# Two transformer blocks on one core: value projection from the raw input, router logits from the raw residual, and the affine part moved behind the gather

## The chip, the cores and the metric

The kernel runs on one core of a Trainium2 chip. The metric is the time on the device, in microseconds, of one execution. PE is the matrix engine, DVE the vector engine, ACT the scalar engine, POOL the general-purpose engine, and SP the engine whose queue issues the transfers.

## The reference

Input x is 1024 tokens of width D = 1024, in fp32. Two blocks run one after the other.

```python
def rmsnorm(x, g): return x * rsqrt(mean(x*x, -1) + EPS) * g
# block 1
h = rmsnorm(x, attn_pre_norm)
proj = h @ w_in                       # window attention, forget attention, latent attention
qm = rmsnorm(c_q, q_latent_norm) @ w_uq       # c_q: 256 columns of proj
kv = rmsnorm(c_kv, kv_latent_norm) @ w_ukv    # c_kv: 128 columns
x = x + rmsnorm(mixed @ w_out, attn_post_norm)
x = x + rmsnorm((gelu(gate) * up) @ w_down, ffn_post_norm)
# block 2: c is one vector
sh1, sc1, gt1, sh2, sc2, gt2 = split(silu(c) @ w_ada + b_ada)
h = rmsnorm(x, g_mix) * (1 + sc1) + sh1       # windowed attention and a short convolution
x = x + gt1 * (concat(att, conv) @ w_out)
h2 = rmsnorm(x, g_ffn) * (1 + sc2) + sh2
aff = softmax(h2 @ w_router)                  # 16 experts
g, idx = top_k(aff.T, 128)                    # each expert picks its 128 tokens
y = (silu(h2[idx] @ w_gate[e]) * (h2[idx] @ w_up[e])) @ w_down[e] * g
x = x + gt2 * scatter_add(y, idx)
out = rmsnorm(x, g_final)
```

## The kernel before

The activations lie in SBUF as 8 tiles (k) of 128 features by 1024 tokens, tokens along the free axis. Every large product is made in three passes, high x high, low x high and high x low, where a "high" is a copy rounded to fp32r (made on ACT) and a "low" is the rest (a subtraction on DVE or POOL). Each engine has its own program, written out by hand; semaphores alone join them. All transfers but the gathers and scatters are issued by SP, in order.

**Start.** SP loads x in four pairs of tiles (L507), then the value weights (L509), then the modulation weights in 8 tiles (`adaA`). ACT squares x, DVE sums the squares (`squares`, `sums`, L1950), PE makes the mean with a matrix of ones (`mean(0)`, L682), ACT the root, DVE the inverse on the diagonal of a matrix (L1963), PE spreads that over all partitions (`spread(0)`, L689), and only then DVE scales x (L2006), ACT rounds it (L1430) and DVE takes the rest (L2011). PE's order is: `keep_clock(10)`, 20 products whose result is not used (L675); mean; bias flips (L788); spread; the modulations of tiles 0 to 3 (L770, 32 rows); the value products (L812 to L814, 8 units of token block by half, 24 products each); the modulations of tiles 4 to 7; then the 13 tiles of the input projection (L826 to L828). DVE and ACT each empty one half of a projection tile. POOL makes the low part of the value weights in one piece (L2611).

**Latent norms.** The sums of squares of the latent columns are averaged at projection tiles 3 and 5 and spread at 4 and 6.

**Output projection and router.** The second output projection has 16 parts of 24 products (`output_part2`, L947 to L949); parts 0 to 7 are the first half of the tokens, 8 to 15 the second. DVE adds each to the residual (`gated`, L2437). The normed, scaled and shifted input hT is made on DVE and ACT (L2444, L1694). From it PE makes the logits (L1210), and for each of the 8 token blocks two transposes, one of the residual and one of hT (`row_turn`, L1201). ACT empties those (L1835) and SP stores them to DRAM as rows (L609), to which the routed row's affinities are added. After the softmax DVE ranks them in 16 rounds of 8 (L2487), finds each token's position and writes the indices; POOL gathers each expert's 128 rows (L2758).

**Experts.** An expert is 24 items: 8 k-tiles of gate, of up and of down. An item is 6 products of 128x512 (L1299 to L1301). ACT rounds its weight tile into one of RING = 4 buffers (`part_high`, L1875), DVE takes the rest (`part_low`, L2543); PE's item waits for that, and ACT's next write into the buffer waits for PE's item four before. Within an expert, PE turns the next expert's gathered rows ahead of its first up item (`turn_rows`, L1308), and ACT and DVE turn them into operands ahead of their own item 4:

```python
def columns(e, b):                      # ACT, at i == 4
    act_e.wait_ge(s_xt, e + 1)
    act_e.activation(x_hi[:, b]..., banks(4, D), ACT.Copy).then_inc(s_xhi, 1)
...
if not last and i == 4:                 # DVE
    columns_low(e + 1, 1 - b)
```

## Time and profile before

| what | value |
| --- | --- |
| median of 3 runs | 2589.3 us (2589.24 to 2589.64) |
| profiled execution, its own time | 2590.66 us |
| its span, first to last instruction | 2588.8 us |
| mean granted clock of PE | 0.975 |
| busy share: PE, DVE, ACT, POOL | 95%, 62%, 48%, 27% |
| chain that ended last | PE 72%, issue 11%, DVE 8%, POOL 4%, ACT 4% |

A share of busy time is a mean over the whole program. The stage from about 2000 us on, the experts, is 23% of the span and has other limits than the projections before it, so each stage is read by itself. In the rows further down, times count from the start of the span; a row of the timeline has start, duration, engine, line, operation, output and inputs, shapes, the number of instructions it groups, and in brackets how long the engine was idle before, and what ended that.

### The profile page before, as it was taken

How to read it: one execution, taken by the hardware profiler on the slowest of the kernel's cores; microseconds unless marked ns; L12 is line 12 of the kernel's file. 1: busy time of each engine (PE TensorE's matmuls, PEld its weight loads, DVE VectorE, ACT ScalarE, POOL GpSimd, SP SyncE). 2: the span in 40 equal slices, each digit the busy share in tenths (PEclk: the TensorE clock that was granted, in tenths of full speed). 3: DMA queues.
4: the chain of work that ended last, by engine and by line, in shares of the span. 5: the costliest groups of instructions: out<-in, count | busy, mean ns of one | idle time of the engine just before them, and what ended most of it. 6: DMA issues, size and time to landing. Idle time of an engine off the chain costs nothing.

```text
span 2588.8 us, 32543 instructions
## 1 busy us (share of the span) xinstructions
PE 2452.7 (95%) x11378; PEld 1918.5 (74%) x11378; DVE 1610.7 (62%) x2439; ACT 1254.0 (48%) x1852; POOL 689.7 (27%) x396
## 2 busy tenths in 40 slices
PE   8999899999999999999999999999997999999996
PEld 5787567777778788777778777765764888888884
DVE  5032887756643367665432635588247999999997
ACT  4121554434543323343433421376344888888886
POOL 1222100113434477334456222121220110111100
PEclk9999999999999999999999999999998999999997
DMA  7100000022222264222223111000138999999996
GB/s 279 49 33 17 34 1 1 1 114 82 82 82 97 97 230 146 80 82 84 95 98 114 66 65 49 33 1 1 67 117 316 402 387 386 397 386 390 396 361 219
DMA packets 86601, 384.06 MB, mean 148 GB/s; under 512 B 7980, under 2 KB 9180, under 8 KB 71520
## 3 DMA queue, kind: packets, MB, share of 16 engines
q1 hardware_dynamic: 81744, 365.25, 37.5%
q0 software_dynamic: 4752, 17.43, 2.5%
q8 instruction: 63, 1.03, 0.2%
q14 instruction: 42, 0.34, 0.0%
HBM read 361.60 MB, written 21.05 MB: 148 GB/s over the span
## 4 chain that ended last, share of the span: by engine, by line
PE 72%; issue 11%; DVE 8%; POOL 4%; ACT 4%; DMA 1%; POOLq 0%; SPq 0%; DVEq 0%; ACTq 0%
PE ps L947 10%; PE ps L949 10%; PE ps L948 10%; PE ps L1299 7%; PE ps L1301 7%; PE ps L1300 7%; POOL w_lo L2667 4%; PE ps L756 3%; PE ps L902 2%; PE ps L826 2%; PE ps L828 2%; PE ps L827 2%; PE ps L748 2%; PE ps L1149 1%; PE ps L770 1%
## 5 line engine op out<-in xcount | busy, mean ns | idle before, releaser
L2667 POOL TENSOR_TENSOR w_lo<-arena,w_hi 128x1024 fp32r<-128x1024 f32 x188 | 462.7, 2462 | 746.4 <-ACT w_hi L1544 742.2
L2543 DVE TENSOR_TENSOR e_lo<-arena,e_hi 128x1024 fp32r<-128x1024 f32 x384 | 454.2, 1221 | 45.4 <-ACT e_hi L1875 34.1
L1875 ACT ACTIVATE e_hi<-arena 128x1024 fp32r<-128x1024 f32 x384 | 404.1, 1062 | 103.1 <-PE ps L1301 103.1
L1544 ACT ACTIVATE w_hi<-arena 128x1024 fp32r<-128x1024 f32 x188 | 198.4, 1055 | 362.9 <-PE ps L949 362.9
L947 PE MATMUL ps<-h_hi,w_hi 128*128 128x512 f32 x848 | 342.6, 404 | 21.4 <-POOL w_lo L2667 11.7
L948 PE MATMUL ps<-h_lo,w_hi 128*128 128x512 f32 x848 | 335.9, 396 | 0.0
L949 PE MATMUL ps<-h_hi,w_lo 128*128 128x512 f32 x848 | 335.9, 396 | 0.0
L947 PEld LDWEIGHTS ps<-h_hi,w_hi 128*128 128x128 f32 x848 | 162.9, 192 | 66.1 <-issue 28.1
L1299 PE MATMUL ps<-e_hi,x_hi 128*128 128x512 f32 x512 | 202.2, 395 | 3.0 <-DVE x_lo L2538 2.6
L1301 PE MATMUL ps<-e_lo,x_hi 128*128 128x512 f32 x512 | 199.5, 390 | 0.0
L1300 PE MATMUL ps<-e_hi,x_lo 128*128 128x512 f32 x512 | 199.3, 389 | 0.0
L949 PEld LDWEIGHTS ps<-h_hi,w_lo 128*128 128x128 f32 x848 | 162.6, 192 | 35.3
L948 PEld LDWEIGHTS ps<-h_lo,w_hi 128*128 128x128 f32 x848 | 163.3, 193 | 33.6 <-issue 1.2
L2234 DVE SCALAR_TENSOR_TENSOR arena<-ps,cols,arena 128x511 f32<-128x511 f32 x88 | 63.8, 746 | 198.0 <-ACT arena L1631 198.0
L947 PE MATMUL ps<-a_hi,w_hi 128*128 128x512 f32 x352 | 138.0, 392 | 3.5 <-DVE arena L2248 3.5
L948 PE MATMUL ps<-act_lo,w_hi 128*128 (+1 forms) x352 | 137.6, 391 | 0.0
L949 PE MATMUL ps<-a_hi,w_lo 128*128 128x512 f32 x352 | 137.6, 391 | 0.0
L1950 DVE TENSOR_TENSOR arena<-arena 128x512 f32<-128x512 f32 (+2 forms) x85 | 85.7, 1008 | 72.7 <-ACT arena L1371 68.6
L1631 ACT ACTIVATE arena<-ps,cols 128x512 f32<-128x512 f32 x88 | 63.6, 773 | 136.5 <-PE ps L949 135.7
L2781 POOL DMA_INDIRECT residual_rows<-arena,tiny x15 | 27.3, 1821 | 356.7 <-DVE arena L2550 356.7
L1299 PEld LDWEIGHTS ps<-e_hi,x_hi 128*128 128x128 f32 x512 | 96.2, 188 | 22.4 <-DVE x_lo L2538 2.9
L1301 PEld LDWEIGHTS ps<-e_lo,x_hi 128*128 128x128 f32 x512 | 96.1, 188 | 20.3
(372 smaller groups left out, 5094.4 us busy)
## 6 DMA issues: line engine op xcount, KB each, us to landing
arena<-in_w_up SPq DMA_DIRECT2D x108, 1024.0 KB, 7.0
arena<-in_w_down SPq DMA_DIRECT2D x86, 1024.0 KB, 7.2
arena<-in_w_gate SPq DMA_DIRECT2D x64, 1024.0 KB, 9.4
arena<-in_w_in SPq DMA_DIRECT2D x18, 1024.0 KB, 4.8
arena<-in_w_out SPq DMA_DIRECT2D x16, 1024.0 KB, 4.7
arena<-in_w_ada SPq DMA_DIRECT2D x12, 1024.0 KB, 12.1
arena<-in_w_ada SPq DMA_DIRECT2D x24, 512.0 KB, 6.8
routed_rows<-arena SPq DMA_DIRECT2D x8, 520.0 KB, 2.6
```

The costliest lines, as they stand in the source:

```text
L756: i = pe.matmul(ps[:, value_bank(w, isdense(w)), 0:HD], probsT[w % 2][:, j * P:(j + 1) * P], group(w)[2](w % 8, j), start=(j == 0), stop=( ...
L947: pe.matmul(out, w_hi[:, q, w], hi, start=start, stop=False)
L948: pe.matmul(out, w_hi[:, q, w], lo, start=False, stop=False)
L949: return pe.matmul(out, w_lo[:, q, w], hi, start=False, stop=stop)
L1299: pe.matmul(out, hi[:, k, :], e_hi[:, r, w], start=(k == 0), stop=False)
L1300: pe.matmul(out, lo[:, k, :], e_hi[:, r, w], start=False, stop=False)
L1301: m = pe.matmul(out, hi[:, k, :], e_lo[:, r, w], start=False, stop=(k == KT - 1))
L1544: act_e.activation(w_hi[:, q, :], slot[c][:, q * D:(q + 1) * D], ACT.Copy).then_inc(s_whi, 1)
L1875: act_e.activation(e_hi[:, (2 * sl + a) % RING, :], slot[sl][:, a * D:(a + 1) * D], ACT.Copy).then_inc(s_ehi, 1)
L1950: v.tensor_tensor(sm[:, 0:n], sm[:, 0:n], sqs[k % 2][:, 0:n], ALU.add).then_inc(s_add, 1)
L2543: v.tensor_tensor(e_lo[:, r, :], slot[sl][:, a * D:(a + 1) * D], e_hi[:, r, :].bitcast(F32), ALU.subtract).then_inc(s_elo, 1)
L2667: gp.tensor_tensor(w_lo[:, q, :], slot[c][:, q * D:(q + 1) * D], w_hi[:, q, :].bitcast(F32), ALU.subtract).then_inc(s_wlo, 1)
```

## The change

It has three parts.

**First input projection from the raw input.** SP loads the value weights first, then x. ACT rounds x times the norm's gain, without the inverse root, and DVE takes the rest in one operation. PE runs 6 times 2 unused products in place of 10 times 2, then the value products, k outermost over four units, then the other four; mean and spread stand among these. The inverse root is applied where results are emptied: as a scale of one number a row for the values (`v_tile`), and as a product with a row for the 13 tiles (`first_tile`), whose both halves DVE now empties. The low part of the value weights is made in two halves, on DVE and POOL. All modulations and flips come behind the values.

**Latent norms** are averaged and spread one tile later.

**Router.** The logits come from the raw residual, with router weights scaled by the gain; the inverse root and the shift of the logits are applied on 128x64 values (`affinity_shifted`). hT is gone, and so are `spread` and the 16 scaling and 16 shifting operations. A token block needs one transpose (`row_turn`), emptied twice on ACT, raw and times the inverse root (`rows_out`). The rows gathered are normed but lack gain and shift: `columns` on ACT applies those in 8 operations before the rounding, for each expert. The unused products ahead of the first expert are gone; parts of `second_gate` stand there. Some weights load earlier.

```diff
+            sp.dma_start(wv, T["w_in_v"]).then_inc(extra, 16)
             for i in range(4):
...
+                sp.dma_start(x0_pairs[i], T["xT"][:, 2 * i:2 * i + 2, :]).then_inc(xl[i], 16)
...
-            keep_clock(10)
-            mean(0)
-            pe.wait_ge(s_bias, 16)
-            bias_turned(range(2))
-            spread(0)
-            bias_turned(range(2, 4)).then_inc(s_flip, 1)
+            keep_clock(6)
...
+            pe.wait_ge(s_n1, 2)
+            for k in range(KT):
+                if k == KT // 2:
+                    pe.wait_ge(s_ilo, 1)
+                pe.wait_ge(s_nhi, k + 1)
+                for u in range(4):
+                    value_product(u // 2, u % 2, k, False)
+                pe.wait_ge(s_h, k + 1)
+                for u in range(4):
+                    m = value_product(u // 2, u % 2, k, True)
...
-                if t in (3, 5):
-                    mean(1 if t == 3 else 2)
                 if t in (4, 6):
-                    spread(1 if t == 4 else 2)
+                    mean(1 if t == 4 else 2)
+                if t in (5, 7):
+                    spread(1 if t == 5 else 2)
...
+            def logits(half, k):
+
+                pe.wait_ge(eva if k % 2 else evv, T_OUT2 + 4 * half + k // 2 + 1)
...
+                m = pe.matmul(ps[0:NE, 7, :], wr_scaled[:, k, :], xT[:, k, half * HALF:(half + 1) * HALF], start=(k == 0), stop=(k == KT - 1))
...
-            output_part2(KT, {4: lambda: mean(12)})
-            output_part2(KT + 1, {2: lambda: spread(12)})
-            for i in range(2):
-                output_part2(KT + 2 + i, {1: lambda: row_turn(2 * i), 5: lambda: row_turn(2 * i + 1)})
-            output_part2(KT + 4, {0: lambda: logits(0), 6: lambda: logit_rows(0)})
-            output_part2(KT + 5, {5: lambda: row_turn(4)})
-            output_part2(KT + 6, {1: lambda: row_turn(5), 5: lambda: row_turn(6)})
-            output_part2(KT + 7, {1: lambda: row_turn(7)})
+            output_part2(KT, {4: lambda: mean(12), 6: shift_logits})
+            output_part2(KT + 1)
+            output_part2(KT + 2, {0: first_logits, 5: lambda: logit_rows(0)})
+            output_part2(KT + 3, {4: lambda: logits(1, 0)})
+            output_part2(KT + 4, {2: lambda: row_turn(0), 6: lambda: logits(1, 1)})
+            output_part2(KT + 5, {0: lambda: logits(1, 2), 3: lambda: row_turn(1), 6: lambda: logits(1, 3)})
+            output_part2(KT + 6, {1: lambda: logits(1, 4), 5: lambda: row_turn(2)})
+            output_part2(KT + 7)
+            for k in range(5, KT):
+                logits(1, k)
+            mean(13)
+            logit_rows(1)
...
-            fill(1)
+            second_gate(6)
             pe.wait_ge(s_cna, 1)
...
+            def first_input_high(k):
+
+                act_e.wait_ge(xl[k // 2], 16)
+                act_e.activation(n_hi[:, k, :], x0[k], ACT.Copy, scale=col("attn_pre", k)).then_inc(s_nhi, 1)
...
+                act_e.activation(raw[:, 0:D], banks(row_bank(t), D), ACT.Copy).then_inc(s_rte, 1)
...
+                act_e.activation(normed[:, 0:D], banks(row_bank(t), D), ACT.Copy, scale=rms[t // 4][:, t % 4:t % 4 + 1]).then_inc(s_rte, 1)
...
             def columns(e, b):
 
                 act_e.wait_ge(s_xt, e + 1)
-                act_e.activation(x_hi[:, b].rearrange("p a b -> p (a b)"), banks(4, D), ACT.Copy).then_inc(s_xhi, 1)
+                for k in range(KT):
+                    act_e.activation(hx[:, k * P:(k + 1) * P], ps[:, 4 + k // 4, (k % 4) * P:(k % 4 + 1) * P], ACT.Identity,
+                                     bias=mod[:, 24 + k, 0:1], scale=gsc[:, 2, k:k + 1]).then_inc(s_hx, 1)
+                act_e.wait_ge(s_hx, KT * e + KT)
+                act_e.activation(x_hi[:, b].rearrange("p a b -> p (a b)"), hx, ACT.Copy).then_inc(s_xhi, 1)
...
+                    v.scalar_tensor_tensor(n_lo[k], x0[k], col("attn_pre", k), n_hi[:, k, :].bitcast(F32), ALU.mult, ALU.subtract).then_inc(s_h, 1)
...
+            vc_.link(v.tensor_scalar(flog[0:4], flog[0:4], fbias[0:4], None, ALU.add))
...
+                vc_.link(v.tensor_tensor(aff[:, part, :], lg, rms[half][:, 0:4].unsqueeze(2).to_broadcast([P, 4, NE]), ALU.mult))
+                vc_.link(v.tensor_tensor(aff[:, part, :], aff[:, part, :], lg_shift.unsqueeze(1).to_broadcast([P, 4, NE]), ALU.add))
...
-            gp.wait_ge(s_dg, 1)
             gp.wait_ge(s_ihi, 1)
-            gp.tensor_tensor(v_lo[:], wv, v_hi[:].bitcast(F32), ALU.subtract).then_inc(s_ilo, 1)
+            gp.tensor_tensor(v_lo[:, KT // 2:KT], wv[:, KT // 2:KT], v_hi[:, KT // 2:KT].bitcast(F32), ALU.subtract).then_inc(s_ilo, 1)
```

What PE does first, in the kernel before (`ps<-const` are the unused products, `arena` here the squares, the diagonal or the modulation weights):

```order
L675 MATMUL ps<-const 128x512 x10
L682 MATMUL ps<-const,arena 128x1 [waits squares_summed]
L682 MATMUL ps<-const,arena 128x1 x7
L788 MATMUL ps<-arena,const 128x512 [waits bias_loaded]
L788 MATMUL ps<-arena,const 128x512
L689 MATMUL ps<-arena,const 128x128 [waits inverse_root_on_diagonal]
L689 MATMUL ps<-arena,const 128x128 x7
```

and after the change, where `g_hi` is the rounded input and `n_lo` its low part:

```order
L688 MATMUL ps<-const 128x512 x6
L812 MATMUL ps<-v_hi,g_hi 128x384 [waits first_input_high_ready,first_value_weights_split_or_bias_copied]
L813 MATMUL ps<-v_lo,g_hi 128x384
...
L811 MATMUL ps<-v_hi,n_lo 128x384 [waits first_input_low_ready_or_normalised]
L811 MATMUL ps<-v_hi,n_lo 128x384 x3
```

The mean, the flips and the spread no longer stand ahead of the value products; a wait for the first low part does, after eight products.

PE behind the last output part, in the kernel before:

```order
L1201 MATMUL ps<-const,arena 128x128 [waits tile_evacuated_act,tile_evacuated_dve]
L1201 MATMUL ps<-const,arena 128x128 x7
L682 MATMUL ps<-const,arena 128x1 [waits squares_summed,row_tile_evacuated]
L682 MATMUL ps<-const,arena 128x1 x3
L689 MATMUL ps<-arena,const 128x128 [waits inverse_root_on_diagonal]
L689 MATMUL ps<-arena,const 128x128 x3
L1201 MATMUL ps<-const,arena 128x128 x8
L1210 MATMUL ps<-arena 16x512 [waits shifted,late_params_loaded,row_tile_evacuated]
L1210 MATMUL ps<-arena 16x512 [waits shifted] x7
```

and after the change:

```order
L1252 MATMUL ps<-arena 16x512 [waits tile_evacuated_act]
L695 MATMUL ps<-const,arena 128x1 [waits squares_summed]
L695 MATMUL ps<-const,arena 128x1 x3
L1260 MATMUL ps<-const,arena 128x16 [waits logits_copied]
L1260 MATMUL ps<-const,arena 128x16 x3
L1234 MATMUL ps<-const,arena 128x128 [waits tile_evacuated_act,tile_evacuated_dve]
L1234 MATMUL ps<-const,arena 128x128 x15
```

The logits (L1210, now L1252) wait for the residual's tile and no longer for the mean, the spread and the scaling; the row transposes stand behind the logits' own.

ACT where it takes the next expert's rows out of PSUM, in the kernel before:

```order
L1875 ACTIVATE e_hi<-arena 128x1024 [waits expert_weight_used,slot5_loaded]
L1862 ACTIVATE x_hi<-ps 128x1024 [waits rows_to_columns]
L1875 ACTIVATE e_hi<-arena 128x1024 [waits expert_weight_used,slot6_loaded] x2
```

and after the change:

```order
L1897 ACTIVATE e_hi<-arena 128x1024 [waits expert_weight_used,slot5_loaded]
L1881 ACTIVATE arena<-ps,tiny 128x128 [waits rows_to_columns]
L1881 ACTIVATE arena<-ps,tiny 128x128 x7
L1884 ACTIVATE x_hi<-arena 128x1024 [waits expert_columns_shifted]
L1897 ACTIVATE e_hi<-arena 128x1024 [waits expert_weight_used,slot6_loaded] x2
```

Eight operations stand ahead of the one that was there, and the next weight tile's rounding stands behind them.

## Rows read from the trace of the kernel before

**Rows 1.** The page, busy time of each engine.
```profile
PE 2452.7 (95%) x11378; PEld 1918.5 (74%) x11378; DVE 1610.7 (62%) x2439; ACT 1254.0 (48%) x1852; POOL 689.7 (27%) x396
```

**Rows 2.** The chain of waits, start to latent norms: start, duration, engine, line.
```profile
47.46 0.37 PE ps L812
80.97 13.82 PE ps L770 x32
...
138.54 1.68 PE ps L682 x16
...
152.34 1.98 PE ps L689 x16
```

**Rows 3.** Timeline of the start, on ACT, POOL and DVE.
```profile
9.15 2.00 ACT L1371 ACTIVATE arena<-arena 128x1024 f32<-128x1024 f32 x2 [0.98 <-DMA arena<-in_xT]
...
21.55 1.47 ACT L1404 ACTIVATE v_hi<-arena 128x1536 fp32r<-128x1536 f32 x1
...
27.41 6.67 POOL L2611 TENSOR_TENSOR v_lo<-arena,v_hi 128x3072 fp32r<-128x3072 f32 x1 [26.96 <-DVE arena L1963]
...
33.01 2.28 DVE L2006 SCALAR_TENSOR_TENSOR arena<-arena,cols 128x512 f32<-128x512 f32 x2 [5.69 <-ACT arena L1382]
```

**Rows 4.** Windows: length, busy (count) of PE, PEld, DVE, ACT, POOL; clock; DMA share, GB/s.
```profile
22.00:24.00 2.00, 2.00 (x10) 2.00 (x10) 0.00 (x0) 1.02 (x1) 0.00 (x0) 0.50 1.09 380
...
30.00:32.00 2.00, 2.00 (x14) 1.95 (x13) 0.00 (x0) 0.05 (x1) 2.00 (x1) 0.73 1.03 430
...
2305.00:2339.00 34.00, 34.00 (x158) 27.70 (x157) 31.47 (x30) 28.09 (x29) 4.55 (x5) 1.00 1.02 393
```

**Rows 5.** Timeline of DVE behind the first projection.
```profile
253.12 0.97 DVE L2068 TENSOR_SCALAR arena<-arena 4x1024 f32<-4x1024 f32 x1
```

**Rows 6.** Timeline of the second half of the output projection, on DVE and PE.
```profile
1871.82 0.75 DVE L2437 SCALAR_TENSOR_TENSOR arena<-ps,tiny,arena 128x512 f32<-128x512 f32 x1 [3.30 <-PE ps L949]
...
1902.11 8.45 PE L1210 MATMUL ps<-arena 128*16 128x512 f32 x16 [2.94 <-issue]
...
1936.79 0.75 DVE L2437 SCALAR_TENSOR_TENSOR arena<-ps,tiny,arena 128x512 f32<-128x512 f32 x1 [2.40 <-PE ps L949]
```

**Rows 7.** Timeline from there to the ranking, on DVE and PE.
```profile
1947.87 9.46 PE L1210 MATMUL ps<-arena 128*16 128x512 f32 x16 [3.23 <-ACT arena L1694]
...
1960.99 0.42 DVE L2484 COPY arena<-ps 128x256 f32<-128x256 f32 x1 [0.53 <-PE ps L1245]
```

**Rows 8.** Timeline of the first expert's start, on DVE, PE and ACT.
```profile
1986.67 1.27 DVE L2512 SCALAR_TENSOR_TENSOR arena<-arena,tiny 16x1024 bf16<-16x1024 f32 x1
...
1988.77 1.46 PE L1267 MATMUL ps<-arena,maskbf 16*128 16x512 bf16 x6
...
2001.69 0.50 PE L1299 MATMUL ps<-e_hi,x_hi 128*128 128x512 f32 x1 [2.63 <-DVE x_lo L2538]
...
2015.86 1.02 ACT L1862 ACTIVATE x_hi<-ps 128x1024 fp32r<-128x1024 f32 x1
```

**Rows 9.** Timeline of a later expert, around the first up item, on PE and DVE.
```profile
2330.29 1.03 PE L1308 MATMUL ps<-const,arena 128*128 128x128 f32 x8
...
2336.62 0.39 PE L1299 MATMUL ps<-e_hi,x_hi 128*128 128x512 f32 x1
...
2333.69 1.22 DVE L2538 TENSOR_TENSOR x_lo<-ps,x_hi 128x1024 fp32r<-128x1024 f32 x1
2334.82 8.39 DVE L2543 TENSOR_TENSOR e_lo<-arena,e_hi 128x1024 fp32r<-128x1024 f32 x7
```

**Rows 10.** Groups of ACT by form: count, busy, mean ns, idle before; and two rows of its timeline.
```profile
L1631 ACT ACTIVATE arena<-ps,cols 128x512 f32<-128x512 f32 x88 | 63.6, 773 | 136.5 <-PE ps L949 135.7 <-DVE arena L2257 0.8
L1584 ACT ACTIVATE arena<-ps 128x512 f32<-128x512 f32 x12 | 7.1, 592 | 17.3 <-PE ps L949 17.3
...
56.04 0.28 ACT L1414 ACTIVATE arena<-ps 128x128 f32<-128x128 f32 x1 [2.44 <-PE ps L814]
56.21 0.38 ACT L1424 ACTIVATE arena<-ps 128x256 f32<-128x256 f32 x1
```

More of the change, by code:

```diff
@@ new lines, in _ @@
+            for t in range(3):
+                store_rows(t)
+            sp.wait_ge(tps, 2 * (T_OUT2 + 8))
+            for i in (2, 3):
+                gate2_weights(i)
+            expert_weights(0, 0, None, range(2))
+            store_rows(3)
+            expert_weights(0, 0, None, (2,))
+            store_rows(4)
+            expert_weights(0, 0, None, (3,))
+            store_rows(5)
+            expert_weights(1, 0, None, (2,))
+            store_rows(6)
+            expert_weights(1, 0, None, (3,))
@@ L789, in bias_turned, with value_product @@
                 return m
-            keep_clock(10)
-            mean(0)
-            pe.wait_ge(s_bias, 16)
-            bias_turned(range(2))
-            spread(0)
-            bias_turned(range(2, 4)).then_inc(s_flip, 1)
+            keep_clock(6)
+            def value_product(t, h, k, low):
+                out, rows = ps[:, VALUE_BANK[t] + h, 0:384], slice((2 * t + h) * P, (2 * t + h + 1) * P)
+                if low:
+                    return pe.matmul(out, n_lo[k][:, rows], v_hi[:, k, :], start=False, stop=(k == KT - 1))
+                pe.matmul(out, n_hi[:, k, rows], v_hi[:, k, :], start=(k == 0), stop=False)
+                return pe.matmul(out, n_hi[:, k, rows], v_lo[:, k, :], start=False, stop=False)
+            pe.wait_ge(s_n1, 2)
[8 more added lines that the diff above has]
+                    m = value_product(u // 2, u % 2, k, True)
+                    if k == KT - 1:
+                        m.then_inc(tps, 1)
+            for t in range(2, 4):
+                for h in range(2):
+                    if t == 3:
+                        pe.wait_ge(eva if h else evv, 1)
+                    for k in range(KT):
+                        if (t, h, k) == (2, 1, 4):
+                            mean(0)
+                        if (t, h, k) == (3, 0, 4):
+                            spread(0)
+                        value_product(t, h, k, False)
+                        m = value_product(t, h, k, True)
+                    m.then_inc(tps, 1)
             pe.wait_ge(s_silu, 1)
@@ L1909, in _ @@
             part_high(3, 1, 1, 0, True)
-            count(5, 6)
+            count(5, 2)
             count(6, 0)
```

469 lines of the change are left out of this document (222 added, 247 removed).

## The prediction

> **What bounds the kernel now.** I read the page first: PE is busy 95% of the span [rows 1], so whatever gives time must take work off PE or close one of its gaps. Then the chain of waits, which says where the gaps are. At the start the chain runs through PE, with the value products from 47.46 and the last modulations from 80.97 for 13.82, so the first tile of the input projection starts at 94.79 [rows 2]. Then the timeline, engine by engine, around the three places the change touches, and the windows for the granted clock. The clock is at its lower level (0.50) from 22 to 24 us, behind an idle stretch of PE, and between the levels (0.73) from 30 to 32 [rows 4]. In the experts PE has no gap at all, 34.00 of 34 us, but DVE has 31.47 of 34 and ACT 28.09 [rows 4]: each expert is PE's, with two engines that can lose little.
>
> **The change part by part.** Plus is time gained.
>
> *1. The start.* Now PE reaches the value products only after the norm and half of the modulations. After the change they start when the weights and the first x are there. The first pair of x tiles is seen by ACT at 9.15 [rows 3]; the value weights (1.5 MB) now go ahead of it and cost 1.6 million bytes at 430 GB/s [rows 4], 3.7 us, so x lands at about 12.8. ACT rounds the weights in two pieces of 1.47 [rows 3] from about 10.4, when they land by the same rate, to 13.4, and the first x tile, some 1.0, to 14.4. PE's 12 unused products end about then. So PE starts at 14.4.
>
> From there it has to do the value products, 80.97 - 47.46 = 33.5; the modulations, 2 x 13.82 = 27.6; flips, 8 products at 13.82/32 = 0.43, 3.5; mean 1.68 and spread 1.98 [rows 2]. Together 68.3. Waits: POOL makes the second half of the low weights, half of 6.67 [rows 3], from 13.4 to 16.75. POOL worked from 27.41 to 34.08, and DVE, whose operation of the same kind and size is 0.75 elsewhere [rows 6], took 2.28 for two from 33.01 [rows 3]; I read it as DVE held up by POOL. So the first low part comes at about 18.0 and PE, done with its eight products at 15.9, waits 2.1. Another 0.7 for the diagonal. And the idle microseconds cost clock: the low level from 22 us on lasted some 9 us behind 4 us of idling, here I take half of that, 5 us at half speed, 2.5. Sum 14.4 + 68.3 + 2.1 + 0.7 + 2.5 = 88.0 against 94.79: **+6.8**. Bounds: no wait and no clock loss gives +12, both waits twice as long and 4.5 of clock loss +2.
>
> *2. Behind the first projection.* DVE empties both halves of each tile, 2 x 0.7 in 5.4 us of PE work, which hides it, since DVE does nothing else there. The forget bias is now an operation of its own in DVE's chain that PE waits for: the row of that form is 0.97 [rows 5], of which I count half, since other work lies beside its end: **-0.5**. The latent norms a tile later: 0, the chain shows PE on projection tiles around both mean and spread [rows 2] with no wait, and the latent product that uses them is six tiles on. Without that cover it would cost the root and the diagonal, about 3.
>
> *3. Second half of the output projection.* From the emptying that ends part 7 to the last, before: 1936.79 - 1871.82 = 65.0 [rows 6]. After: 8 parts of 24 products at 0.227 (24 x 8 x 0.227 = 43.6), three row transposes at 0.8, mean 0.9, 13 logit products of two passes at 0.43 (11.2), the shift logits 1.4, logit rows 0.4, and 1.5 for the changes between kinds, as the 65.0 also leaves: 61.4. Before it had five more transposes, a spread, five fewer logit products, and 2.94 of waiting with slower logits behind it [rows 6]. One new stall: the second transpose waits for the first block's two copies on ACT, 1.0. **+2.6**, between +1 and +5.
>
> *4. From the last output part to the ranking.* Before: 1960.99 - 1936.79 = 24.2 [rows 6, 7], in which mean, root, spread, eight scalings and eight shifts stand one behind the other, then logits at a sunken clock (9.46) [rows 7]. After, behind the last emptying (0.75): the last logit product 0.9, then the steps that before lie between the logits' end at 1957.33 and 1960.99, 3.7 [rows 7], two more small DVE operations 0.5, one load of ACT's table that stands in the open 1.3, and 0.2 of slack: 7.3. **+16.9**, between +14.5 and +17.5. The ranking itself is the same.
>
> *5. The first expert.* Before: positions ready at 1986.67 + 1.27 = 1987.94, first product at 2001.69: 13.75 [rows 8]. The unused products that kept the clock are gone, PE idles through the ranking, so the position products, 1.46 before [rows 8], take twice that and those that follow likewise: 1.5. Then the eight new operations of ACT (price below) 2.9. So 18.2, -4.5. The first items run at the lower clock for some 4.6 us, as behind the idle stretch at the start: -2.3. **-6.8**, between -3.5 (clock kept) and -9.
>
> *6. Eight operations an expert.* No row has a 128-wide ACT operation with pointers for bias and scale. The nearest: with both pointers 512 wide 773 ns, without 592, so pointers cost 0.18; 128x128 without pointers is 0.28 long, and what follows starts 0.17 later [rows 10]. So 0.46 long, 0.35 apart: 7 x 0.35 + 0.46 = 2.89 (bounds: 1.5 if the pointers cost nothing behind one another, 3.7 if nothing overlaps). In the first expert's copy for the second, at 2015.86 [rows 8], ACT is late already behind its first items, so all is lost: **-2.9**.
>
> *7. The fourteen others.* Follow the row group of the later expert. The transposes start at 2330.29 and end at about 2331.2 [rows 9]. Then, after: hop 0.25 and eight operations 2.89 to 2334.4, the wait on their own semaphore 0.06, rounding 1.05 to 2335.5, DVE's low part of it 1.14 apart (its starts are 2333.69 and 2334.82 [rows 9]), to about 2336.65 and, since it stands ahead of item 4's low weights, those 1.22 more: 2337.9. PE wants item 4 at 2336.62 [rows 9]. A stall of **1.3**. The next weight tile's rounding stands queued behind ACT's eight and ends at 2336.6, in time for DVE, so the path through DVE decides. Seven low parts take 8.39 against 7 x 1.36 = 9.5 of PE [rows 9], so DVE gains 0.2 an item and does not stall again. 14 x 1.3 = **-18.2**, bounds 0 and -24.
>
> The Trainium skill, page "ScalarE: Activation LUTs", section "What ACT_TABLE_LOAD costs", has for an activation 186 ns and 0.833 ns an element, 93 ns more for each pointer operand, and 93 ns of overlap. An estimate by that page is eight operations in 3.2 us rather than 2.9, and by it the sum would be 4 us slower. The rows here agree in size (0.28 for a plain 128x128), and the sum above goes by the rows.
>
> *Transfers.* After the last output part the queue has 13.7 MB to move: two loads of second gate weights 2.1, four of the first gate 4.2, two of up 2.1, stores of five token blocks 5.3. At 393 GB/s [rows 4] that is 35 us. The gather needs the last store, and comes 7.3 + 27.0 + 4.3 = 38.6 after the last output part. So the stores are hidden, barely: below about 370 GB/s they are not.
>
> **Sum.** +6.8 - 0.5 + 2.6 + 16.9 - 6.8 - 2.9 - 18.2 = -2.1. The profiled execution took 2590.66, 1.4 above the median of 2589.3, so the sum is 2592.8 as a profiled execution and **2591.4** against the median. A measurement of this kernel can tell 0.2%, 5.2 us, from no change, so the likeliest outcome is "the same", out of large gains and an equal loss.
>
> **Rivals.**
>
> *A, the forecast.* 2591.4, own range 2584 to 2598. Chance 0.42.
>
> *B, the ring of four weight buffers covers the eight operations.* If they start 0.19 or less apart, the chain of part 7 ends by item 4's time and the stalls are gone; the 0.17 of a plain copy [rows 10] is there already. For it: pipelined operations may hide the reading of pointers. Against it: pairs with pointers 512 wide show the full difference. Parts 6 and 7 then cost about nothing: 2591.4 - 21.1 = 2570. Chance 0.24, faster.
>
> *B2, the start has no hold-up*, DVE is not held by POOL and the clock stays: +12 for +6.8, and some of the stalls smaller: 2586, chance 0.10.
>
> *C, DVE cannot make it up.* Slower. Each expert puts DVE's chain 1.8 later, against 34.00 - 31.47 = 2.5 of free time an expert [rows 4]. If more than 1.3 of that lies where DVE must wait for ACT's next tile anyway, the delay meets the gated product or the low part of the turned tile later in the same expert, and PE loses the whole 1.8: 14 x 0.5 = 7.0 more, 2598.4. It decides from a second stall of over 0.1. Against it: the 8.39 for seven. Chance 0.14.
>
> *D, the stores come late.* Slower. At 330 GB/s, below the 370 where it decides, the last store ends some 6 late, the gather and all behind it too: 2597. For it: 380 to 430 GB/s is all that the busiest windows show, and stores and loads share the queues. Against it: the early loads of up need nothing. Chance 0.10.
>
> **How the numbers follow.** B is all faster, 0.24; of A 0.05 is faster, 0.27 the same, 0.10 slower; B2 0.03 and 0.07; C 0.02 the same, 0.12 slower; D 0.01 and 0.09. So faster 0.32, same 0.37, slower 0.31. The range takes in B with 4 for an unsure size, and C with as much: 2566 to 2602.
>
> **What the profile would show.** Part 1: PE's first value product at 14.4, the first L826 counterpart at 88. Parts 3 and 4: 61 to 63 us for the half, 7.3 to the ranking. Part 5: 18.2 to the first expert product and a clock under 0.9 behind it. Parts 6 and 7: ACT's eight operations 0.35 apart, and PE idle 1.3 ahead of item 4 of each expert, ended by DVE's low weights. I am wrong if PE shows no gap there, or if the operations stand 0.2 apart, or if a second gap follows in each expert.

## The result and the profile after

The changed kernel takes 2596.9 us (median of 8 runs, 2592.8 to 2602.1), the kernel before 2589.3 in the same comparison (8 runs, 2584.8 to 2590.2). The ratio is 1.003, with a 95% interval of 1.0018 to 1.0041: **slower by 7.7 us, 0.3%**. The forecast was 2591.4 in a range of 2566 to 2602. The time lies in the range, but the likeliest outcome was "the same", and it is slower, just beyond the 0.2% (5.2 us) that the prediction took a measurement to tell. Slower had a chance of 0.31 there, and the own range of rival A, 2584 to 2598, holds the time. One execution of one experiment below took 2798.2 us at a mean granted clock of 0.84 where its others have 0.97 to 0.98; it is left out of every comparison.

The profiled executions are 11.5 us apart (spans 2600.3 and 2588.8), more than the medians: the one of the changed kernel is its slowest run. So the places below are read stage by stage, and their sum is the profile's, not the medians'.

From the page after: span, busy time, and the chain by engine.

```profile
span 2600.3 us, 32442 instructions
...
PE 2442.7 (94%) x11296; PEld 1904.6 (73%) x11296; DVE 1599.0 (61%) x2415; ACT 1273.8 (49%) x1937; POOL 692.0 (27%) x396
...
PE 69%; issue 10%; DVE 10%; ACT 6%; POOL 4%; DMA 0%; SPq 0%; POOLq 0%; DVEq 0%; ACTq 0%
```

PE does 10.0 us less of work than before [rows 1], yet the span is longer: its share of the chain falls from 72% to 69%, and DVE's and ACT's rise, from 8% and 4% to 10% and 6%. The work taken away was on the path, and new waits are too.

The two spans cut into the same ten stages, from the timelines. Forecast and measured are what the change gains; minus is lost. The term of -0.5 for what lies behind the first projection stands at the third stage:

| stage | before | after | forecast | measured |
| --- | --- | --- | --- | --- |
| to the first input projection product | 94.72 | 87.92 | +6.8 | +6.8 |
| its 13 tiles, first to last product | 150.19 | 153.37 | 0 | -3.2 |
| to the emptying that ends output part 7 | 1626.91 | 1628.09 | -0.5 | -1.2 |
| second half of the output projection | 64.97 | 63.45 | +2.6 | +1.5 |
| to the ranking | 24.20 | 7.07 | +16.9 | +17.1 |
| ranking and positions | 26.95 | 26.95 | 0 | 0.0 |
| to the first expert product | 13.75 | 21.83 | -4.5 | -8.1 |
| to the second expert's transposes | 11.04 | 12.39 | -2.3 | -1.4 |
| to the third expert's | 35.86 | 40.23 | -2.9 | -4.4 |
| 13 further, and the rest | 540.21 | 559.00 | -18.2 | -18.8 |

**Start.** Timeline of the changed kernel's start on PE, DVE and POOL.

```profile
14.81 0.41 PE L812 MATMUL ps<-v_hi,g_hi 128*128 128x384 f32 x1
...
18.51 1.50 PE L811 MATMUL ps<-v_hi,n_lo 128*128 128x384 f32 x4 [2.07 <-DVE n_lo L2020]
...
14.70 8.54 DVE L2020 SCALAR_TENSOR_TENSOR n_lo<-arena,cols,g_hi 128x1024 fp32r<-128x1024 f32 x5 [0.65 <-ACT g_hi L1441]
...
13.71 3.66 POOL L2665 TENSOR_TENSOR v_lo<-arena,v_hi 128x1536 fp32r<-128x1536 f32 x1 [13.26 <-ACT v_hi L1436]
```

PE starts at 14.81 (forecast 14.4), waits 2.07 for the first low part (forecast 2.1), and its four products behind the wait take 1.50, where later groups of four take 0.85: the clock has fallen, as forecast. Nine traces of this case have this start unchanged (the changed kernel's and eight of the runs below), and in them the wait of 1.6 to 2.1 is always there, but the fall is not: in six the first tile of the projection starts at 87.6 to 88.1, and in three, where the clock stays up, at 86.0 to 86.3. One of those three, the run without the eight operations:

```profile
18.40 0.96 PE L811 MATMUL ps<-v_hi,n_lo 128*128 128x384 f32 x4 [2.07 <-DVE n_lo L2016]
```

So 1.7 of the stage differs from one execution to the next.

**Latent norm.** The chain of waits behind the fourth tile.

```profile
142.64 1.08 PE ps L790 x16
143.71 2.29 PE ps L695 x16
146.01 0.64 PE ps L862
146.64 0.43 PE ps L863
```

The mean takes 2.29 in place of 1.68 [rows 2], and the products behind it 0.43 each in place of 0.23. The granted clock in windows (length, busy of PE, PEld, DVE, ACT, POOL; clock; DMA share, GB/s):

```profile
140.00:146.00 6.00, 6.00 (x45) 5.28 (x43) 1.38 (x2) 1.06 (x1) 2.13 (x1) 0.92 0.01 3
146.00:152.00 6.00, 6.00 (x16) 4.70 (x16) 1.43 (x2) 0.27 (x1) 0.22 (x1) 0.51 0.00 0
```

PE is busy all the time, and at the lower level (0.51) from 146 to 152. The prediction had costed this step at nothing.

**Router.** The same two kinds of row as before [rows 6, 7], the emptying of parts 7 and 15 and the copy that begins the ranking.

```profile
1869.38 0.75 DVE L2484 SCALAR_TENSOR_TENSOR arena<-ps,tiny,arena 128x512 f32<-128x512 f32 x1 [3.30 <-PE ps L985]
...
1932.83 0.75 DVE L2484 SCALAR_TENSOR_TENSOR arena<-ps,tiny,arena 128x512 f32<-128x512 f32 x1 [3.29 <-PE ps L985]
...
1939.90 0.42 DVE L2538 COPY arena<-ps 128x256 f32<-128x256 f32 x1 [0.53 <-PE ps L1289]
```

**First expert.** Timeline of PE from the positions to the first product.

```profile
1966.99 2.71 PE L1317 MATMUL ps<-arena,maskbf 16*128 16x512 bf16 x6 [5.66 <-DVE arena L2567]
1969.64 3.78 PE L1303 MATMUL ps<-arena,tiny 128*128 128x512 f32 x4
1973.35 1.03 PE L1317 MATMUL ps<-arena,maskbf 16*128 16x512 bf16 x2
1974.31 3.78 PE L1303 MATMUL ps<-arena,tiny 128*128 128x512 f32 x4
1978.02 1.03 PE L1317 MATMUL ps<-arena,maskbf 16*128 16x512 bf16 x4
...
1988.68 0.79 PE L1341 MATMUL ps<-e_hi,x_hi 128*128 128x512 f32 x1 [7.08 <-DVE x_lo L2593]
```

The positions take 2.71 for 1.46 [rows 8], as forecast. But two pieces of the second gate's product (L1303, 3.78 each at the lower clock) stand between them, and ACT's counts of positions, which must be done before ACT turns to the first rows, wait behind. The size of this, too, differs between executions: in three of the runs below (without the eight operations, as plain copies, one operation a rounding) the clock is up again at the second piece, whose products then take 0.59 each in place of 1.06.

**A later expert**, on PE, ACT and DVE.

```profile
2334.27 1.03 PE L1350 MATMUL ps<-const,arena 128*128 128x128 f32 x8
...
2341.86 0.50 PE L1341 MATMUL ps<-e_hi,x_hi 128*128 128x512 f32 x1 [1.10 <-DVE e_lo L2598]
...
2335.44 2.88 ACT L1881 ACTIVATE arena<-ps,tiny 128x128 f32<-128x128 f32 x8
2338.36 1.06 ACT L1884 ACTIVATE x_hi<-arena 128x1024 fp32r<-128x1024 f32 x1
...
2339.45 1.23 DVE L2593 TENSOR_TENSOR x_lo<-arena,x_hi 128x1024 fp32r<-128x1024 f32 x1 [1.70 <-ACT x_hi L1884]
2340.59 2.35 DVE L2598 TENSOR_TENSOR e_lo<-arena,e_hi 128x1024 fp32r<-128x1024 f32 x2
```

The eight operations take 2.88 (forecast 2.89), DVE idles 1.70 for them, and PE has a gap of 1.10 ahead of item 4. The waits of PE from 2040 us to the end (total, times, longest):

```profile
PE ps L1341 <- DVE e_lo L2598: 15.4, 14, 1.1
```

Fourteen gaps, one an expert. The distance between experts grows by 1.40 (36.61 for 35.21), more than the gap's 1.10: a product's row is 0.39 long and the next one usually starts 0.23 behind its start, so a gap of 1.10 in the rows is 1.26 lost from start to start, and the first product behind it takes 0.11 more.

### The profile page after: what moved, and what is told of

It is laid out like the page before. It is cut to its first block, busy times and chain, and to the rows that moved or that the text cites. A ratio compares the mean times of both kernels' runs of the same rounds, so it can differ in the third digit from the quotient of the medians.

```text
span 2600.3 us, 32442 instructions
## 1 busy us (share of the span) xinstructions
PE 2442.7 (94%) x11296; PEld 1904.6 (73%) x11296; DVE 1599.0 (61%) x2415; ACT 1273.8 (49%) x1937; POOL 692.0 (27%) x396
## 4 chain that ended last, share of the span: by engine, by line
PE 69%; issue 10%; DVE 10%; ACT 6%; POOL 4%; DMA 0%; SPq 0%; POOLq 0%; DVEq 0%; ACTq 0%
PE ps L983 10%; PE ps L985 10%; PE ps L984 10%; PE ps L1341 6%; PE ps L1343 6%; PE ps L1342 6%; POOL w_lo L2722 3%; PE ps L769 3%; PE ps L938 2%; PE ps L862 2%; PE ps L863 2%; PE ps L864 2%; ACT arena L1881 2%; PE ps L761 2%; PE ps L1185 1%
## 5 line engine op out<-in xcount | busy, mean ns | idle before, releaser
L1341 PE MATMUL ps<-e_hi,x_hi 128*128 128x512 f32 x512 | 205.2, 401 | 25.6 <-DVE e_lo L2598 18.5
L1341 PEld LDWEIGHTS ps<-e_hi,x_hi 128*128 128x128 f32 x512 | 96.8, 189 | 50.9 <-DVE e_lo L2598 24.8
## 6 DMA issues: line engine op xcount, KB each, us to landing
arena<-in_w_ada SPq DMA_DIRECT2D x12, 1024.0 KB, 10.6
```

The lines of the kernel that those rows point to most:

```text
L1341: pe.matmul(out, hi[:, k, :], e_hi[:, r, w], start=(k == 0), stop=False)
```

## The experiments

Single executions of one kernel lie 3 to 12 us apart. The medians of the kernel before, taken anew for each group of runs, lie within 1.4 (2589.3 to 2590.6). So a difference of 3 us between the medians of two changed kernels shows little, and verdicts here rest on the stages of the traces first. How much a stage can scatter: the stretch from the end of the projection to output part 7, which no experiment touches, takes between 1623.6 and 1631.6 in these traces. All diffs are cut to the lines that matter.

### The eight operations

**Without them** (gain and shift left out of the experts' input; DVE's low part, too, reads the rows from PSUM):

```diff
-                for k in range(KT):
-                    act_e.activation(hx[:, k * P:(k + 1) * P], ps[:, 4 + k // 4, (k % 4) * P:(k % 4 + 1) * P], ACT.Identity,
-                                     bias=mod[:, 24 + k, 0:1], scale=gsc[:, 2, k:k + 1]).then_inc(s_hx, 1)
-                act_e.wait_ge(s_hx, KT * e + KT)
-                act_e.activation(x_hi[:, b].rearrange("p a b -> p (a b)"), hx, ACT.Copy).then_inc(s_xhi, 1)
+                act_e.activation(x_hi[:, b].rearrange("p a b -> p (a b)"), banks(4, D), ACT.Copy).then_inc(s_xhi, 1)
```

> The changed kernel with the eight operations gone: the gathered rows are rounded straight from PSUM, as before, so gain and shift are left out of the experts' input (nothing else). My theory: PE's gap ahead of item 4 (1.1 us, 14 times), what it costs in the second expert (4.4) and the 2.9 ahead of the first expert all go, 14 x 1.4 + 4.4 + 2.9 = 27, so 2597 - 27 = 2570, and experts 35.2 us apart as before instead of 36.6. Rival: the gaps come from later weights or rows (transfers), then they stay and the time is above 2590.

Measured: 2572.1 (ratio to before 0.9928, 0.9913 to 0.9943). Experts are 35.21 apart again, the third starts 35.86 behind the second, and PE's list of waits from 2040 us on has no e_lo row. The 14 gaps are these operations' and nothing else's. The whole is 24.8 less than the changed kernel, where 27 was expected.

**As plain copies**, without pointers (gain and shift left out likewise):

```diff
-                    act_e.activation(hx[...], ps[...], ACT.Identity, bias=mod[:, 24 + k, 0:1], scale=gsc[:, 2, k:k + 1]).then_inc(s_hx, 1)
+                    act_e.activation(hx[...], ps[...], ACT.Copy).then_inc(s_hx, 1)
```

> The eight operations stay, as plain copies of 128x128 without pointers for bias and scale (gain and shift are left out of the experts' input). If their spacing decides, they stand 0.17 apart in place of 0.35, the group takes 1.5 in place of 2.9, the gap of 1.1 a expert closes, and the time is 2597 - 14 x 1.2 - 3 - 1.4 = 2576. If the hop over their own semaphore and the changed source of the low part cost more than the spacing, half of the gap stays and it is 2585.

Measured: 2576.7 (0.9950, 0.9934 to 0.9965). ACT's timeline has

```profile
2316.84 1.44 ACT L1881 ACTIVATE arena<-ps 128x128 f32<-128x128 f32 x8
```

1.44 for eight where the pointers make it 2.88, the experts are 35.21 to 35.27 apart, and PE has no gap ahead of item 4. At 0.17 apart the ring covers the operations, at 0.35 it does not. That agrees with the threshold of rival B (0.19), which no run tests more closely; B was wrong about the price.

**In another order.** PE turns the next expert's rows ahead of the fifth down item of the expert before; ACT does two operations ahead of each of items 0 to 3.

```diff
+                    if turn and k == 4:
+                        turn_rows(e + 2, b)
...
+                    if not last and i < 4:
+                        if i == 0:
+                            act_e.wait_ge(s_xt, e + 2)
+                        columns_shifted(e + 1, range(2 * i, 2 * i + 2))
                     if not last and i == 4:
-                        columns(e + 1, 1 - b)
+                        columns_high(e + 1, 1 - b)
```

> All the work stays, in another order: the rows of the next expert are turned on PE in the middle of the down items of the expert before, and ACT makes the eight operations two at a time ahead of four roundings, then the rounding of the rows where it was. If the stall is one of order (one block of 2.9 us in front of a queued rounding, with 6 us of ACT free an expert), the gaps go: 2597 - 20 (fourteen experts) - 2 (second expert) = 2575. If it is one of capacity (DVE at 31.5 of 34), the gaps only move and the time stays within 4 of 2597.

Measured: 2594.6 (1.0010, 1.0001 to 1.0020). The theory of order expected 2575; the time lies where the theory of capacity put it, within 4 of 2597. Experts are 36.28 apart, and PE's waits from 2040 us on read

```profile
PE ps L1341 <- DVE e_lo L2614: 8.5, 14, 0.6
```

The gap only shrank from 1.1 to 0.6. DVE's timeline shows why:

```profile
2328.84 1.23 DVE L2614 TENSOR_TENSOR e_lo<-arena,e_hi 128x1024 fp32r<-128x1024 f32 x1 [0.76 <-ACT e_hi L1909]
2330.49 1.23 DVE L2614 TENSOR_TENSOR e_lo<-arena,e_hi 128x1024 fp32r<-128x1024 f32 x1 [0.42 <-ACT e_hi L1909]
2332.13 1.23 DVE L2614 TENSOR_TENSOR e_lo<-arena,e_hi 128x1024 fp32r<-128x1024 f32 x1 [0.41 <-ACT e_hi L1909]
```

With two operations a step, ACT needs 1.64 a weight tile where PE takes 1.36. Three small idle times of DVE make 1.6 us, just ahead of the place where it has most to do (the output, the rows' low part). Neither of the two theories had that. The next run shows that it was order after all, and that this new order was still a wrong one.

**One operation ahead of each of eight roundings**, and the rows' rounding and low part at item 8, the first item that reads them (the diff is against the run before):

```diff
-                    if not last and i < 4:
+                    if not last and i < KT:
                         if i == 0:
                             act_e.wait_ge(s_xt, e + 2)
-                        columns_shifted(e + 1, range(2 * i, 2 * i + 2))
-                    if not last and i == 4:
+                        columns_shifted(e + 1, range(i, i + 1))
+                    if not last and i == KT:
```

> The run with the early turn still had a gap of 0.6 an expert, with DVE waiting for ACT's roundings 0.4 to 0.8 at a time while ACT did two operations ahead of each. Here one operation stands ahead of each of eight roundings (0.95 + 0.35 against 1.36 of PE), and the rounding of the rows and its low part come at item 8. If order is all, experts are 35.2 apart as before, and the time is 2597 - 20 - 2 = 2575. If DVE's load is the limit, they stay over 36.

Measured: **2576.3** (0.9942, 0.9927 to 0.9957), all of the computation in place. ACT's timeline:

```profile
2318.48 0.44 ACT L1890 ACTIVATE arena<-ps,tiny 128x128 f32<-128x128 f32 x1
2318.87 1.06 ACT L1909 ACTIVATE e_hi<-arena 128x1024 fp32r<-128x1024 f32 x1
2319.84 0.44 ACT L1890 ACTIVATE arena<-ps,tiny 128x128 f32<-128x128 f32 x1
2320.23 1.06 ACT L1909 ACTIVATE e_hi<-arena 128x1024 fp32r<-128x1024 f32 x1
```

Pairs start 1.36 apart, PE's own pace. Experts are 35.27 apart: 0.06 an expert is left of 1.40. DVE's load is no limit, which answers rival C. Two things differ from the run before, the pairs made single and item 8 for item 4; no run separates them.

### The latent norms

**Put back by one tile** in the changed kernel (`mean` at tiles 3 and 5, `spread` at 4 and 6, and ACT's and DVE's halves of it):

```diff
-                if t in (4, 6):
-                    mean(1 if t == 4 else 2)
-                if t in (5, 7):
-                    spread(1 if t == 5 else 2)
+                if t in (3, 5):
+                    mean(1 if t == 3 else 2)
+                if t in (4, 6):
+                    spread(1 if t == 4 else 2)
```

> Only the latent norms are put back one projection tile earlier, as before the change. In the changed kernel the 16 small products of the first latent mean now stand right behind the 16 small ones that turn the modulations, and some 20 full products behind them run at twice their time, which was not so before. If that neighbourhood costs the clock, this gains 3 us (2594) and the products behind the mean take 0.23 again. If the lower clock there comes from elsewhere, no change (2597).

Measured: 2607.6 (1.0061, 1.0047 to 1.0075), 10.7 slower, a plain miss. PE's wait from 120 to 250 us, and its chain:

```profile
PE ps L695 <- DVE tiny L1979: 5.1, 1, 5.1
```
```profile
131.45 3.20 DVE arena L1973
135.04 3.54 PE ps L695 x16
```

The mean comes before DVE has summed the squares. DVE now empties both halves of every tile, so the sum stands behind the second half of the tile (1.39). In the kernel before, DVE emptied only the first half and began the sum 3.9 before PE came to the mean. The sum itself takes 3.2 here and 1.2 there: it begins at 131.45, beside an operation of POOL that runs from 131.22 to 133.56, as in the start (below). So without this step the first part of the change costs 5.1 of waiting and the clock as well (13 tiles in 159.5 in place of 153.4).

**The turned modulations one tile ahead** of the mean, so that the two groups of 16 small products stand apart:

```diff
                     pe.wait_ge(s_row, 1)
-                if t == 4:
                     columns(rowA, 2 * KT, 1)
```

> The changed kernel, with the 16 small products that turn the modulations moved one tile ahead, away from the first latent mean. If neighbourhood costs the clock, the 13 tiles take 150.2 as before the change in place of 153.4, and the time falls by 3 to 2594. If the clock falls at the mean anyway, 153 and no change.

Measured: 2597.1 (median of seven; 1.0024, 1.0014 to 1.0035) against 2596.9, where 2594 was expected: no change in the medians. In the trace the 13 tiles take 150.27, and the products behind the mean take 0.23 again but for the first:

```profile
131.92 1.07 PE ps L790 x16
133.00 0.43 PE ps L862
...
144.14 1.68 PE ps L695 x16
145.82 0.35 PE ps L862
```

**The kernel before with the later norms**:

> The kernel before, with nothing but the latent norms one projection tile later, so that the first latent mean stands right behind the 16 small products that turn the modulations. If that neighbourhood costs the clock, the projection's 13 tiles take 150.2 + 1.6 to 3.2 and the products behind the mean run at about 0.43 for a while. If not, 150.2 and no change of the time (2590).

Measured: 2590.7 (0.9998, 0.9989 to 1.0008), 13 tiles in 150.16. The same neighbours, and no fall of the clock:

```profile
150.19 1.07 PE ps L777 x16
151.26 1.88 PE ps L682 x16
153.13 0.34 PE ps L826
```

So neighbourhood by itself did not cost the clock in this trace. All eight traces in which the two stand together behind the new start show a fall, which costs 1.6 in four and 3.2 in four; the three with the two apart (the run above and the two combined kernels below) show none, 150.2 to 150.3. What else it takes stays open. In the medians the gain is not seen; 1.6 to 3.2 is within what their executions scatter.

### The start

**The second half of the value weights' low part on DVE**, behind two low parts of the input, in place of POOL:

```diff
-            gp.wait_ge(s_ihi, 1)
-            gp.tensor_tensor(v_lo[:, KT // 2:KT], ..., ALU.subtract).then_inc(s_ilo, 1)
...
+            first_input_low(range(2))
+            v.wait_ge(s_ihi, 1)
+            v.tensor_tensor(v_lo[:, KT // 2:KT], ..., ALU.subtract).then_inc(s_ilo, 1)
```

> The second half of the value weights' low part is made on DVE behind the first two low parts of the input, and no more on POOL. If POOL's operation (3.66 from 13.71) holds DVE up, the first low part now ends at 16 in place of 18.4, PE's gap of 2.07 behind its first eight products goes, and with it the lower clock from 18.5 to 22 (some 1.7): the first tile of the input projection starts at 84.5 in place of 88 and the time is 3.5 lower. If DVE was late for another reason (its own operation is slow on fp32r output), the gap stays and the time grows by the 1.8 moved to DVE.

Measured: 2594.0 (1.0009, 0.9999 to 1.0019), 2.9 less than the changed kernel, with an interval that still touches its (1.0018 to 1.0041). In the trace the projection starts at 84.08 in place of 87.92, 3.8 earlier; against the three traces in which the clock stayed up (86.0 to 86.3) it is 2.0 earlier, the wait alone. PE and DVE:

```profile
16.32 0.85 PE L811 MATMUL ps<-v_hi,n_lo 128*128 128x384 f32 x4
...
14.72 2.48 DVE L2020 SCALAR_TENSOR_TENSOR n_lo<-arena,cols,g_hi 128x1024 fp32r<-128x1024 f32 x2 [0.66 <-ACT g_hi L1441]
17.12 1.75 DVE L2024 TENSOR_TENSOR v_lo<-arena,v_hi 128x1536 fp32r<-128x1536 f32 x1
```

Two low parts take 2.48 where POOL is idle, and the wait and the slow products are gone. That the same operation, begun at 14.70 beside POOL's, reached PE only at 18.5 was POOL's doing. The Trainium skill, page "SBUF — State Buffer", section "SBUF: two separate sides", has DVE and GpSimd share one pair of ports, held for a whole instruction, where the DVE operation has two inputs in SBUF, as this one has, and the GpSimd one reads SBUF. The traces agree: POOL's operation ends at 17.37 (13.71 + 3.66), and the first low part is with PE 1.14 later, about what one takes where POOL is idle (1.24).

### The first expert

**The second gate's last pieces ahead of the positions**:

```diff
-            for k in range(3, 6):
+            for k in range(3, KT):
                 second_gate(k)
...
-            second_gate(6)
             pe.wait_ge(s_cna, 1)
             positions(3, 2)
-            second_gate(7)
```

> The last two pieces of the second gate's product (7.6 us on PE at the lower clock) are moved from between the position products to ahead of them, into PE's idle time during the ranking. My forecast had 18.2 from the positions to the first expert product, 21.8 was measured. If these pieces hold up the counts (the third count waits until 1974.4), the 21.8 falls to 18.2 and the time by 3.6, to 2593. If the late row stores or ACT's counts set it, it stays at 21.8.

Measured: 2597.2 (1.0028, 1.0018 to 1.0039) where 2593 was expected, no change in the medians. In the trace the first product comes 18.56 behind the positions in place of 21.83 (forecast 18.2), but the second expert's transposes only 1.8 earlier, since the first items are slower (13.8 in place of 12.4):

```profile
1960.81 2.29 PE L1317 MATMUL ps<-arena,maskbf 16*128 16x512 bf16 x6 [2.36 <-DVE arena L2565]
...
1979.22 0.80 PE L1339 MATMUL ps<-e_hi,x_hi 128*128 128x512 f32 x1 [5.42 <-DVE x_lo L2591]
```

Nearly half of what the shorter wait gave (3.3) was taken back: more products of the first items run at the lower level (0.63 each) before it rises. Both kernels idle ahead of the items (5.42 here, 7.08 there), so why it rises later here is open.

**With four unused products ahead of the positions** (a loop of four as in L675, eight in the trace, before the wait for the positions; the rest as in the run before):

> As the run before, with four products of unused results on PE ahead of the position products, to keep the clock through the end of the ranking. If the clock is what makes the rest (forecast 1.5 in the positions, 2.3 in the first items), the stretch falls to 16.7 and the first eight items from 12.4 to about 11, and the time is 2590. Rival: PE idles for 7 us while ACT makes the first expert's operand anyway, and the clock is low again when the items begin; then only the 1.5 is gained, 2592.

Measured: 2595.1, the interval of which (1.0009 to 1.0028) meets that of the run before (1.0018 to 1.0039). The rival was right that the clock is low again when the items begin:

```profile
1964.48 3.60 PE L1322 MATMUL ps<-const 128*128 128x512 f32 x8
1968.01 1.46 PE L1317 MATMUL ps<-arena,maskbf 16*128 16x512 bf16 x6
...
1985.53 0.79 PE L1341 MATMUL ps<-e_hi,x_hi 128*128 128x512 f32 x1 [5.42 <-DVE x_lo L2593]
```

The positions take 1.46 again, but begin 1.2 after they could (at 1966.78), and PE idles for 5.42 ahead of the items, which begin at the lower level (0.63 a product). Of the 1.5 that the rival left nothing is seen in the stage: the first product comes 18.7 behind the positions, for 18.6 without the unused products.

**All repairs together**: one operation a rounding, value weights on DVE, the modulations apart, gate pieces and four unused products ahead.

> All repairs together: one operation a rounding with the early turn, the second half of the value weights' low part on DVE, the modulation's small products one tile ahead, the second gate and four unused products ahead of the positions. If the terms add: 2576.3 - 3.8 - 2.3 - 5 = 2565, 25 below the kernel before. If they overlap (a start that ends earlier meets transfers or the next wait), it stays above 2570.

Measured: 2570.8 (0.9923, 0.9910 to 0.9937). 5.5 less than the spread operations alone, where 11 was expected, and within the rival's "above 2570", so the terms do not add in full; the profiled execution, 2566.8, is its fastest. The first product comes 18.6 behind the positions. POOL's gather still starts 0.35 behind its index, released by a row store.

**Without the unused products, and two loads of up weights behind the last stores** (against the run before; the loop of four goes too):

```diff
             store_rows(5)
-            expert_weights(1, 0, None, (2,))
             store_rows(6)
-            expert_weights(1, 0, None, (3,))
             store_rows(7)
+            expert_weights(1, 0, None, (2, 3))
```

> All repairs as in the run before, without the four unused products (they ended 1.2 after the positions were ready and the clock fell again behind them), and with the last two loads of the first expert's up weights behind the last row stores instead of between them. If the stores end late (in the changed kernel the gather starts 1.2 after its indices are there, released by a store), the gather now starts 0.15 behind its indices, the first product comes 17 behind the positions in place of 18.6, and the time is 2570.8 - 1.6 - 1.2 = 2568. If the copies of rows on ACT and their buffers set the pace of the stores, not the weights between them, the gather starts as late as before.

Measured: **2565.7** (0.9908, 0.9892 to 0.9925), 24 below the kernel before, the best of all. The first product comes 17.7 behind the positions, 0.9 earlier than in the run before. That is all that the traces show of the 5.1 between the two medians: the profiled executions are the slowest of this kernel and the fastest of the one before, 0.8 apart. The rest is not explained, and the two edits are not tested apart. The gather in the changed kernel and here:

```profile
1970.75 0.19 POOL L2812 COPY tiny<-tiny 128x1 uint32<-128x1 uint32 x1 [47.29 <-DMA routed_rows<-arena]
```
```profile
1961.04 0.19 POOL L2825 COPY tiny<-tiny 128x1 uint32<-128x1 uint32 x1 [45.81 <-DVE tiny L2595]
```

It was released by a store, 1.2 behind DVE's index at 1969.5, and now follows the index by 0.17. Rival D was real, with 1.2 and not 6, and in the changed kernel it lay beside the longer wait for the counts. ACT's copies still come 5.04 apart, held by their buffers, so the loads between the stores only set the last landing.

## Why the prediction was right, and where it was wrong

- **Start, +6.8.** Right in the sum and in its terms: 14.8 for 14.4, wait 2.07 for 2.1, the clock's fall 1.7 for 2.5, the wait for values to be emptied 0.3 for the 0.7 put down to the diagonal, and POOL as the cause, which the run with DVE alone shows. That the sum came out to the tenth is luck: without the fall, as in three of nine traces, it is +8.5. With POOL's hold-up gone it is +10.6, near the +12 of rival B2.
- **Latent norms, 0.** The step that failed by its cause. I read in the old chain that PE was busy on both sides, and took the later place for free. The later place has a reason, that DVE now empties both halves in between: in the earlier place PE waits 5.1 and the tiles take 6.1 longer. And the later place put two groups of small products together, with 3.2 lost to the clock in this execution and 1.6 in half of the eight traces with that order.
- **Second half of the output, +2.6, measured +1.5.** The term mis-sized is the work: PE waits only 0.50, so it works 62.9 and not 61.4. From start to start, the logit products take 11.8 (one group of eight 6.97, five of 0.96) for 11.2, the shift logits 1.7 for 1.4, and the changes between kinds, seen as products of the output that stand more than 0.227 apart beside them, about 2.3 for 1.5.
- **To the ranking, +16.9, measured +17.1.** Right: 7.07 for 7.3.
- **First expert, -6.8, measured -9.5** (-8.1 and -1.4). The step named "positions to first product, 18.2" left out the two gate pieces of 3.78 among the positions. They stood in the change's order, and I had counted them as done by then. Without them it is 18.56; with them, but the clock up at the second, it is 20.0.
- **Second expert, -2.9, measured -4.4.** The delay of 2.9 was passed on, as PE's gap of 3.09, and products at the lower clock behind it (0.43 from start to start, from 2012.16 to 2015.15) added the rest. The prediction had no term for what a gap of 3 us costs in clock.
- **Fourteen experts, -18.2, measured -18.8.** Right, with its path: 2.88 for 2.89 of ACT (the terms given, 7 x 0.35 + 0.46, make 2.91), a stall of 1.10 for 1.3 ahead of item 4, ended by DVE's low weights. That removing the operations, or their pointers, removes the stall is shown.
- **Rival D.** Its mechanism is there, with 1.2 us for the forecast 6. Its own figures do not give the 6: 13.7 MB in 38.6 us is 355 GB/s and not 370, and at 330 GB/s the last store would end 2.9 late.

The errors nearly all had one sign, against the change: 3.2 + 0.7 + 1.1 + 2.7 + 1.5 + 0.6 - 0.2 = 9.6 in the profiled executions. Of these, 0.7 (the untouched stretch), half of the 3.2 and some 1.8 of the 2.7 come and go between executions of one kernel. In the medians 5.5 remain (2596.9 for 2591.4). So the range was hit because three of the four largest terms were right (start, ranking, fourteen experts). The others were nearly all too hopeful, and the width of the range took that up.

## What to carry to other kernels

An engine with 6 us free in 34 can still not take one block of 2.9 in front of a queue whose buffers hold 4 tiles: cut such work to the consumer's pace, one piece per tile, and start it early enough that its last piece is done when the consumer comes to it. Starting it early alone was not enough: in pairs it still cost 1.07 an expert. Here the same work in eight pieces turned a loss of 7.7 us into a gain of 14, and of 24 with the other repairs. Where a step is moved, count what every engine does between its new neighbours, and read the new order on PE for products that now stand in front of a waited-for one, even if they were meant to fill idle time.

## What was not expected of the hardware

- An operation of ACT on 128x128 with pointers for bias and scale is 0.35 from start to start, without them 0.17 (2.88 and 1.44 for eight). The estimate of 0.35, put together from wider operations with pointers and a plain one of this width, held.
- The clock fell with PE busy throughout, at 16 and 16 products of little length one behind the other (0.51 from 146 to 152), in all eight traces of the new start with this order, and not in the one trace of the kernel before with the same order (2.29 and 1.88 for the same 16 products). The cause is open.
- The clock fell behind an idle stretch of PE of 2.07 in some executions and not in others of the same start (the first four products behind it took 1.50 or 0.96), and did not fall behind the gaps of 1.10 in the later experts.
- Four unused products (3.60 in the trace), which ended 17.5 ahead of the items, did not keep the clock for them: with 5.42 of idling just ahead, the items began at 0.63 a product all the same.
